# Gate and up products of a feed-forward block: both halves of x in one 512-column matmul, summed afterwards by VectorE

## The reference

```
def _swiglu(x, w_in, w_out):
    gate, up = jnp.split(x @ w_in, 2, axis=-1)      # w_in: 1024 x (2 * 2816)
    return (jax.nn.silu(gate) * up) @ w_out         # w_out: 2816 x 1024

x = layernorm(ALPHA * x + 0.5 * _swiglu(x, w_in, w_out))
```

## Time and profile before

| | us |
|---|---|
| median of 3 runs (1444.24 to 1444.84) | 1444.67 |
| the profiled execution | 1442.08 |
| its span, first to last instruction | 1440.3 |
| TensorE matmul busy | 1420.0 (99%) |
| weight loads busy | 1325.7 (92%) |
| VectorE busy | 975.7 (68%) |
| ScalarE busy | 664.2 (46%) |

### The profile page before, as it was taken

The page is one execution under the profiler, slowest core; times in us unless marked ns, Lnnn a source line. Parts: engine busy times, 40 slices in busy tenths (PEclk is TensorE's granted clock), DMA queues, the critical chain, the costliest instruction groups (busy, mean ns, idle before and its releaser), DMA issues.

```text
span 1440.3 us, 23342 instructions
## 1 busy us (share of the span) xinstructions
PE 1420.0 (99%) x10186; PEld 1325.7 (92%) x10186; DVE 975.7 (68%) x1085; ACT 664.2 (46%) x653; POOL 53.6 (4%) x100
## 2 busy tenths in 40 slices
PE   8999999999999999999999999999999999999997
PEld 7999989999999889999879999899999998999985
DVE  4544576889877874545875545868997868545477
ACT  4434435664545444444454344357545464443441
POOL 0410000000000020000100000000000001000000
PEclk9999999999999999999999999999999999999998
DMA  7676545535554586555565655554456365655641
GB/s 264 215 243 197 183 137 185 176 122 202 175 176 147 177 256 202 193 179 179 169 222 190 200 184 199 167 166 163 152 203 171 97 230 177 226 187 193 193 158 59
DMA packets 168055, 263.35 MB, mean 183 GB/s; under 512 B 8959, under 2 KB 101457, under 8 KB 167953
## 3 DMA queue, kind: packets, MB, share of 16 engines
q1 hardware_dynamic: 163616, 249.66, 53.2%
q0 software_dynamic: 4336, 12.20, 2.8%
HBM read 260.77 MB, written 1.05 MB: 182 GB/s over the span
## 4 chain that ended last, share of the span: by engine, by line
PE 93%; DVE 4%; ACT 1%; DMA 0%; SPq 0%; issue 0%; DVEq 0%; ACTq 0%
PE ps L1244 29%; PE ps L1246 28%; PE ps L1245 28%; PE ps L1446 3%; DVE big L896 2%; PE ps L1270 1%; PE ps L1275 1%; PE ps L1272 1%; DVE wlo L771 1%; PE ps L1311 1%; ACT whi L546 1%; DMA raw<-in_ffn_w_in 0%; DVE big L832 0%; PE ps L1545 0%; ACT xhi L582 0%
## 5 line engine op out<-in xcount | busy, mean ns | idle before, releaser
L771 DVE TENSOR_TENSOR wlo<-raw,whi 128x2048 fp32r<-128x2048 f32 x230 | 524.8, 2289 | 304.1 <-ACT whi L546 303.8
L1244 PE MATMUL ps<-xhi,whi 128*128 128x256 f32 x2336 | 658.8, 282 | 2.7 <-DVE S L786 2.7
L1246 PE MATMUL ps<-xhi,wlo 128*128 128x256 f32 x2336 | 656.1, 281 | 0.0
L1245 PE MATMUL ps<-xlo,whi 128*128 128x256 f32 x2336 | 655.9, 281 | 0.0
L546 ACT CAST whi<-raw 128x2048 fp32r<-128x2048 f32 x230 | 438.1, 1909 | 469.9 <-PE ps L1246 445.9
L1244 PEld LDWEIGHTS ps<-xhi,whi 128*128 128x128 f32 x2336 | 441.6, 189 | 5.8 <-DVE wlo L771 3.1
L1245 PEld LDWEIGHTS ps<-xlo,whi 128*128 128x128 f32 x2336 | 441.5, 189 | 1.5
L1246 PEld LDWEIGHTS ps<-xhi,wlo 128*128 128x128 f32 x2336 | 441.5, 189 | 0.0
L1244 PE MATMUL ps<-whi,bh 128*128 128x512 f32 x368 | 146.5, 398 | 0.0
L1246 PE MATMUL ps<-whi,blo 128*128 128x512 f32 x368 | 145.1, 394 | 0.0
L1245 PE MATMUL ps<-wlo,bh 128*128 128x512 f32 x368 | 144.7, 393 | 0.0
(11 more groups left out here) (241 smaller groups left out, 1208.1 us busy)
## 6 DMA issues: line engine op xcount, KB each, us to landing
raw<-in_ffn_w_in SPq DMA_DIRECT2D x172, 512.0 KB, 4.9
raw<-in_w_in SPq DMA_DIRECT2D x140, 512.0 KB, 4.5
raw<-in_ffn_w_out SPq DMA_DIRECT2D x88, 512.0 KB, 4.4
raw<-in_w_br SPq DMA_DIRECT2D x32, 512.0 KB, 5.4
raw<-in_w_out SPq DMA_DIRECT2D x16, 512.0 KB, 4.4
raw<-in_ple_gate_w SPq DMA_DIRECT2D x16, 512.0 KB, 4.3
gv<-in_ln_g POOLq DMA_DIRECT2D x8, 512.0 KB, 4.8
b_bc<-in_ln_b POOLq DMA_DIRECT2D x8, 512.0 KB, 6.5
```

The costliest lines, as they stand in the source:

```text
L771: nc.vector.tensor_tensor(wlo[:, slot, :], raw[:, source, :], whi[:, slot, :].bitcast(F32), ALU.subtract).then_inc(wlo_made, 1)
L1244: nc.tensor.matmul(dst, a_hi, b_hi, start=start, stop=False, skip_group_check=True)
L1245: nc.tensor.matmul(dst, a_hi, b_lo, start=False, stop=False, skip_group_check=True)
L1246: return nc.tensor.matmul(dst, a_lo, b_hi, start=False, stop=stop, skip_group_check=True)
```

## The change

- `xhi` and `xlo` become halves of one tensor `xhl`. In `gate_up` one matmul of 512 columns takes `[xhi | xlo]` (two runs of 256) against `whi` into a whole bank, and one of 256 columns adds `xhi` against `wlo` into the bank's second half. The bank holds two partial sums of 256 columns. Gate and up of both halves q take banks 0 to 3.
- VectorE adds the two halves of a gate bank and an up bank in one `tensor_reduce` for each q (`sums`), into SBUF (`gsum`, `usum`). silu and the product read these.
- From block 2 on `gate_up` waits for the sums of the block in front, not for its products. Block 1 does q = 1 first and then q = 0, for which it waits for both products of block 0.
- What stood in banks 2 and 3 during the stage moves: the turned hidden block 0 to bank 7, the turned embedding input to bank 6 (with a wait for `pT_made` before `down(0, 0)`).
- In the first FFN `late` moves from between `gate_up(9)` and `gate_up(10)` to behind `down(8, 0)`, with a wait for both products of block 10.

```diff
+        xhl = sb("xhl", [P, 2, KD, T], F32R)
+        xhi, xlo = xhl[:, 0], xhl[:, 1]
+        gsum = S[:, 0, 512:1024].rearrange("p (q t) -> p q t", q=2)
+        usum = S[:, 1, 512:1024].rearrange("p (q t) -> p q t", q=2)
@@ ScalarE, ffn, for j > 0 (q = 1 alike, with 2 * (n - n0 // NFF))
-                    act.wait_ge(gate0_done, n + 1)
-                    nc.scalar.activation(sil[:, 0, :], ps[:, 0, 0:256], ACT.Silu)
+                        act.wait_ge(gsum_made, 2 * (n - n0 // NFF) - 1)
+                        nc.scalar.activation(sil[:, 0, :], gsum[:, 0, :], ACT.Silu)
@@ VectorE, ffn
+                def sums(n, q, g):
+                    if q == 0:
+                        dve.wait_ge(gate0_done, n + 1)
+                    else:
+                        dve.wait_ge(chunk_used, g + 2)
+                    nc.vector.tensor_reduce(S[:, 0:2, 512 + 256 * q:768 + 256 * q],
+                                            ps[:, 2 * q:2 * q + 2, :].rearrange("p u (h t) -> p u t h", h=2),
+                                            AX_X, ALU.add).then_inc(gsum_made, 1)
+                def product_of_sums(n, q):
+                    dve.wait_ge(hlo_made, n)
+                    dve.wait_ge(gsum_made, 2 * (n - n0 // NFF) - 1 + q)
+                    dve.wait_ge(silu_made, 2 * n + q + 1)
+                    nc.vector.scalar_tensor_tensor(hf[:, q, :], sil[:, q, :], 0.5, usum[:, q, :],
+                                                   ALU.mult, ALU.mult).then_inc(h_made, 1)
@@ for j > 0
-                    product(n, 0)
-                    product(n, 1)
+                        for q in range(2):
+                            sums(n, q, g)
+                            product_of_sums(n, q)
@@ TensorE, gate_up
-                        for q in range(2):
-                            if kk == 0:
-                                pe.wait_ge(h_made, 2 * n + q - 1)
+                        for q in (1, 0) if j == 1 and kk == 0 else (0, 1):
+                            if kk == 0 and j > 1:
+                                pe.wait_ge(gsum_made, 2 * (n - n0 // NFF) - 3 + q)
+                            elif kk == 0 and q == 0:
+                                pe.wait_ge(h_made, 2 * n)
                             for u in range(2):
                                 for k in range(4):
-                                    ins = mm3(ps[:, q, 256 * u:256 * u + 256], ... )
+                                    nc.tensor.matmul(ps[:, 2 * q + u, :], w[:, k, u, P * q:P * q + P], xhl[:, :, 4 * kk + k, :],
+                                                     start=kk == 0 and k == 0, stop=False, skip_group_check=True)
+                                    ins = nc.tensor.matmul(ps[:, 2 * q + u, 256:512], v[:, k, u, P * q:P * q + P],
+                                                           xh[:, 4 * kk + k, :], start=False, stop=kk == 1 and k == 3, ...)
@@ TensorE, ffn
+                if middle is not None:
+                    pe.wait_ge(pT_made, n0 // (2 * NFF) + 1)
                 gate_up(NFF - 2)
-                if late is not None:
-                    late()
                 gate_up(NFF - 1)
                 for j in range(NFF - 3, NFF):
                     down(j, 0)
+                    if j == NFF - 3 and late is not None:
+                        pe.wait_ge(h_made, 2 * (n0 + NFF))
+                        late()
```

More of the change, by code:

```diff
@@ L162, in build @@
         xT = wide[:, 0:KD * T].rearrange("p (k t) -> p k t", k=KD)
-        xhi = sb("xhi", [P, KD, T], F32R)
-        xlo = sb("xlo", [P, KD, T], F32R)
+        xhl = sb("xhl", [P, 2, KD, T], F32R)
+        xhi, xlo = xhl[:, 0], xhl[:, 1]
         bh = sb("bh", [P, 2 * KW * T], F32R)
@@ L330, in build @@
         h0_T = sem("h0_T")
+        gsum_made = sem("gsum_made")
         x_in = [sem(f"x_in{t}") for t in range(TT)]
@@ L558, in ffn @@
                     his(g + RING + (1 if j > 0 else -1))
-                    act.wait_ge(gate0_done, n + 1)
-                    nc.scalar.activation(sil[:, 0, :], ps[:, 0, 0:256], ACT.Silu).then_inc(silu_made, 1)
+                    if j == 0:
+                        act.wait_ge(gate0_done, n + 1)
+                        nc.scalar.activation(sil[:, 0, :], ps[:, 0, 0:256], ACT.Silu).then_inc(silu_made, 1)
+                    else:
+                        act.wait_ge(gsum_made, 2 * (n - n0 // NFF) - 1)
+                        nc.scalar.activation(sil[:, 0, :], gsum[:, 0, :], ACT.Silu).then_inc(silu_made, 1)
                     if j == 0:
                         his(g + RING + 1)
-                    act.wait_ge(chunk_used, g + 2)
-                    nc.scalar.activation(sil[:, 1, :], ps[:, 1, 0:256], ACT.Silu).then_inc(silu_made, 1)
+                    if j == 0:
+                        act.wait_ge(chunk_used, g + 2)
+                        nc.scalar.activation(sil[:, 1, :], ps[:, 1, 0:256], ACT.Silu).then_inc(silu_made, 1)
+                    else:
+                        act.wait_ge(gsum_made, 2 * (n - n0 // NFF))
+                        nc.scalar.activation(sil[:, 1, :], gsum[:, 1, :], ACT.Silu).then_inc(silu_made, 1)
                     if j == 0:
@@ L568, in ffn @@
                         act.wait_ge(h0_T, n0 // NFF + 1)
-                        nc.scalar.copy(hhi[0], ps[:, 3, :].rearrange("p (q t) -> p q t", q=2)).then_inc(hhi_made, 1)
+                        nc.scalar.copy(hhi[0], ps[:, 7, :].rearrange("p (q t) -> p q t", q=2)).then_inc(hhi_made, 1)
                         his(g + RING + 2)
@@ L791, in ffn @@
                     los(g + RING + (j > 0))
-                    product(n, 0)
                     if j == 0:
+                        product(n, 0)
                         los(g + RING + 1)
-                    product(n, 1)
+                        product(n, 1)
+                    else:
+                        for q in range(2):
+                            sums(n, q, g)
+                            product_of_sums(n, q)
                     if j == 0 and middle is not None:
@@ L798, in ffn @@
                     dve.wait_ge(hhi_made, n + 1)
-                    src = ps[:, 3, :].rearrange("p (q t) -> p q t", q=2) if j == 0 else hf
+                    src = ps[:, 7, :].rearrange("p (q t) -> p q t", q=2) if j == 0 else hf
                     nc.vector.tensor_tensor(hlo[j % HIDS], src, hhi[j % HIDS].bitcast(F32),
@@ L1199, in embed @@
                     dve.wait_ge(p_turned, l + 1)
-                    nc.vector.tensor_copy(pT, ps[:, 2, :]).then_inc(pT_made, 1)
+                    nc.vector.tensor_copy(pT, ps[:, 6, :]).then_inc(pT_made, 1)
                     dve.wait_ge(phi_made, l + 1)
@@ L1322, in turn_hidden @@
                         for t in range(TT):
-                            ins = nc.tensor.transpose(ps[:, 3, 256 * q + P * t:256 * q + P * t + P],
+                            ins = nc.tensor.transpose(ps[:, 7, 256 * q + P * t:256 * q + P * t + P],
                                                       hf[:, t, P * q:P * q + P], ident)
@@ L1332, in gate_up @@
                         w, v = [a[:, (c + kk) % RING, :].rearrange("p (k u n) -> p k u n", k=4, u=2) for a in (whi, wlo)]
-                        for q in range(2):
-                            if kk == 0:
-                                pe.wait_ge(h_made, 2 * n + q - 1)
+                        for q in (1, 0) if j == 1 and kk == 0 else (0, 1):
[3 more added lines that the diff above has]
+                                pe.wait_ge(h_made, 2 * n)
                             for u in range(2):
                                 for k in range(4):
[L1338 to L1341, removed]
+                                    nc.tensor.matmul(ps[:, 2 * q + u, :], w[:, k, u, P * q:P * q + P], xhl[:, :, 4 * kk + k, :],
+                                                     start=kk == 0 and k == 0, stop=False, skip_group_check=True)
+                                    ins = nc.tensor.matmul(ps[:, 2 * q + u, 256:512], v[:, k, u, P * q:P * q + P],
+                                                           xh[:, 4 * kk + k, :], start=False, stop=kk == 1 and k == 3,
+                                                           skip_group_check=True)
                             if kk == 1 and q == 0:
@@ L1608, in embedding_input @@
                         for t in range(TT):
-                            ins = nc.tensor.transpose(ps[:, 2, 256 * k + P * t:256 * k + P * t + P],
+                            ins = nc.tensor.transpose(ps[:, 6, 256 * k + P * t:256 * k + P * t + P],
                                                       S[:, 3, 256 * t + P * k:256 * t + P * k + P], ident)
```

## The result

| us | before | after |
|---|---|---|
| median, six runs each | 1443.47 (1440.36 to 1444.84) | 1434.44 (1432.55 to 1435.32) |
| profiled execution | 1442.08 | 1432.55 |
| its span | 1440.3 | 1430.7 |
| mean granted clock | 0.995 | 0.998 |

Half of the runs of before are the three known earlier (1444.2 to 1444.8). That is the fairer size of the change. The two profiled spans lie 9.6 us apart, and the part beyond the 6 has to be accounted for too.

A forecast was written before the change was run, and what follows sets the result against it. TensorE was taken to bound the kernel, its matmuls covering 99% of the span. Matmuls -4.5, start -0.2 and stalls +2.1 gave -2.6 us, from 1444.67 to 1442.1 us; the range was 1438.5 to 1449.

The forecast's parts named there:

- the third: `gate_up` matmuls: one weight load less in each of 1280 triples saves 3.5 ns, 4.5 us in all.
- three readings: Saving per `gate_up` triple: 1.7 ns by two means, 4.6 by a `down`'s last matmul, 3.5 by a weight load.
- The nearest row: Last 512-column matmul of a `down`, followed by a 256-column one: saves 4.6 ns a triple, 5.9 us in all.
- The sums: VectorE's two new reduces in each block: 1.22 us each, 98 us in all, hidden in a steady block.
- Rival C: Sums take 2.29 us and stall the ends of the stages, 17.6 us in all, giving 1457.6 us; chance 0.15.
- (a): `gate_up(10)` directly behind `gate_up(9)`: waits 0.2 us for the first sum, four times, 0.8 us in all.
- (b): Block 10 to the norm: later `lo` and residual stall `turn_x`, 0.2 us on average, 0.8 us in all.
- (c): First FFN: `late` waits for both products of block 10, a stall of 0.5 us.
- The start: Block 1: q = 1 runs before the wait for block 0's second product, a gain of 0.2 us.
- The same loss a little later: Behind the start pause, 2.5 us instead of 2.8, half clock still loses about 1.6 us, a little later.
- Rival A: Pair saves 5.9 instead of 4.5 us and the start's half clock, 1.6 us, stays away: 1439.1 us; chance 0.14.
- 3.2 us: `gate_up` saving by the Trainium skill's rule, one fixed cost of 2.5 ns a triple; sum stated as 1443.2.

The follow-up runs named there:

- a2: Changed kernel with only the 512-column matmul of `gate_up` split again into two of 256: 1443.66 us, ratio 1.0013 to the kernel before.
- c2: Changed kernel with the second matmul of the pair also 512 columns wide, adding `xlo` by `wlo`: 1587.34 us, one run.
- b2: Changed kernel with every sum computed twice, one after the other: 1461.05 us, ratio 1.0129 to the kernel before.
- b3: Changed kernel, block 9's first sum ahead of a chunk's subtraction, `late` behind `down(9, 0)`, start pause filled with idle matmuls: 1434.68 us, ratio 0.9948 to the kernel before.
- a1: Changed kernel, unaltered, run again beside the kernel before on the same chip: 1435.5 us, ratio 0.9958.
- a4: Changed kernel with 10 idle matmuls between q = 1 and q = 0 of block 1: 1434.23 us, ratio 0.9951 to the kernel before.
- b1: Changed kernel with `gate_up` waiting for the product of the block in front, not its sum: 1438.13 us, ratio 0.9978 to the kernel before.
- b4: Changed kernel with `xhl` laid out so that the 512 moving columns are one run: 1435.43 us, ratio 0.9955 to the kernel before.
- c1: Changed kernel, unaltered, run once more beside the kernel before on another chip: 1435.01 us, ratio 0.9956.
- c4: The kernel of b3 once more, beside c1 on the same chip: 1433.05 us, ratio 0.9943 to the kernel before.
- a3: Kernel before with 11 idle matmuls into a free bank in its pause at the start: 1440.41 us, ratio 0.9996 to the kernel before.
- b runs: b1, b2, b3 and b4, four variants of the changed kernel run on one chip beside the kernel before: 1438.13, 1461.05, 1434.68 and 1435.43 us.

## Why the prediction was wrong

The direction was right, and the size was not: 9.0 us for the 2.6 forecast. About 3 of the 9.0 don't belong to the change. Against the comparisons on one chip, the median of before lay 2.0 us higher (1443.47 against 1441.5) and that of after 0.6 to 1.1 lower. The other 6 us are 3.4 to 3.8 more than forecast, and the steps below give 2.1 (the pair) + 0.8 (the end of the stage) + 0.5 (four slow blocks) - 0.4 (the handover) = 3.0 of them. Taken step by step:

1. **"I take the third, 4.5 us, which lies between the others": this is the step that failed.** A pair saves 5.2 ns, not 3.5, so 6.6 us, and lies above all three readings; a2 shows that this one matmul carries it. The nearest row gave 4.6 ns, and it was the only one with the order of sizes that the new loop has. I gave it up for a value between it and the mean of `down`, in which 512 follows 512; c2 shows why that mean misleads, since 512 before 512 costs 234.2 ns. The value taken was the load of a stationary operand of 8 columns, read as a weight load saved, and no run shows that a load left out is what is gained: what the 5.2 ns consist of stays open. The 4.6 was also no bound. The 33 such places of before have a mean of 230.0 ns, so it was read rightly, but in the new loop the 512-column matmul takes 229.3 and the 256-column one 117.5 instead of 117.3.
2. **The sums** were priced right (1.22 against 1.218 us) and hidden in steady blocks, with room for another one of each (b2). Rival C's own numbers don't agree with each other: 17.6 us for 1.07 us more is 1.6 for each 0.1 us, not 1.2; b2 has 1.4.
3. **(a) The handover** stalls 0.3 us four times, 1.2 instead of 0.8; 0.08 of the 0.3 is the slower second matmul behind the pause. b3 removes it by taking a subtraction out of the sum's way.
4. **(b) The end of the stage**: VectorE is late, as forecast, and TensorE doesn't notice. From the end of `gate_up(10)` to `turn_x` it takes 13.99 us, as before (13.99 to 14.01), in the last three FFNs; in the first, without `late` and its wait, it takes 0.1 us more. `turn_x` begins its first four transposes when the first half of the normalised x is there, so its slack was larger than the row of the last normalising instruction let it seem. The forecast had 0.8 us too much.
5. **(c) `late`** stalls 0.5 us, as forecast.
6. **The start** gives 0.2 us, as forecast, when the clock stays up. "The same loss a little later" is true of some executions and not of others.
7. **Not foreseen:** four blocks of before (at 45, 62, 756 and 773 us) take 11.39 to 11.40 us at full clock, others 11.26:
```profile
45.41:56.81 11.40, 11.40 (x97) 11.39 (x96) 6.25 (x4) 4.21 (x3) 0.56 (x1) 1.00 0.71 232
```
After has none of them, 0.5 us in all, and neither have the seven other traces of it (a1, a4, b1, b3, b4, c1, c4). a3 has the first two, a2 none, so it is not the number of matmuls; the cause is open, and that the change removed them is not shown.

Measured terms: -6.6 - 0.5 - 0.2 + 1.2 + 0.5 = -5.6 us, against -6.0 and -6.4 in the comparisons on one chip. The 9.6 us between the two profiled spans hold two half-clock stretches more, which before's execution had and after's had not: 1.6 us at the start, where the earlier trace rows saw it, and 1.5 us in the mixing stage, whose code is unchanged (12.92 against 11.37 us for the same 96 matmuls):
```profile
296.00:299.30 3.30, 3.30 (x17) 3.30 (x17) 3.20 (x6) 2.71 (x4) 0.00 (x0) 0.50 0.91 312
```
That leaves 0.9 us, of which 0.5 lies in the rest of the first mixing stage and 0.25 in one stretch of 23.23 against 22.98 us; I have no cause for it. Against them stand 0.2 us that after was late before block 1, by its longer waits for the first weights.

**The range.** It started from a median of 1444.67, some 3 us above what before shows on the same chip as after, and its low end rested on 4.6 ns as a bound. That level may be one of the clock: beside the b runs, executions of before at a granted clock of 0.993 took 1444.5 to 1445.2 us and those at 0.996 1439.6 to 1441.7. With the pair at 5.2 and no loss in (b), the forecast's own arithmetic gives 1439; from the same-chip level of 1441.5 it gives 1436. Rival A named both of the things that came, the dearer saving and the half clock gone, and had 14%; the second is true of some executions only. A slip without weight: with 3.2 us in place of 4.5 the sum comes out at 1443.4, not 1443.2.

## What to carry to other kernels

When a change alters which matmuls follow each other, price them by rows with that order of sizes, not by a mean over another order, and don't call one such reading a bound. Compare medians taken on one chip in one session: here the base alone was worth 3 us. A result that VectorE must first add up out of PSUM was free in a loop with other matmuls behind it, and was paid where two `gate_up` follow each other directly. Free the bank with the earliest reader (the sum, not the product), and let that reader pass longer work on its queue.

## What was unexpected in the hardware

- A 512-column fp32r matmul takes 229.3 ns between two of 256 columns (after), about 230 with one such neighbour (before) and 234.2 between two of 512 (c2). The Trainium skill ("TensorE: Matmul & The Clock Gate", Back-to-back issue gap) has 518 cycles, about 216 ns, for the isolated gap of 512 columns, and names no neighbour and no data type for it; no 512-column fp32r matmul here agrees.
- 512 + 128 + 128 columns take 458 ns, 512 + 256 take 346.8: two short matmuls with a load each cost 111 ns more than one of their joint length.
- A half-clock stretch costs 1.4 to 1.6 us and comes and goes between executions of one kernel: behind the start pause of 2.35 us it is in a1 and b4 and not in c1 or in after's first profile, and it is also seen in the mixing stages, near 295 and 1000 us. In b2 it follows waits of only 2.0 us, three times of three. Six runs of after fall into 1432.6 (clock 0.998), 1434.2 to 1434.7 (0.996) and 1435.0 to 1435.3 (0.995). The same page of the Trainium skill (What's actually happening) says that the moment of transition varies from run to run; here it is also whether the stretch comes at all. So a difference of 1 to 3 us between two profiles of this kernel is to be checked against the clock first.
